# Retention rounds of a hybrid decoder step: one transpose of decayed queries and keys per tile, score and state products of an output bank in groups of four

## The reference

```python
def retention_chunk(S_prev, qkv):
    q, k, v = qkv
    L = q.shape[1]
    ...
    decay = jnp.where(diff[None] >= 0, jnp.exp(lg[:, None, None] * jnp.maximum(diff, 0.0)[None]), 0.0)
    ...
    scores = jnp.einsum('blhd,bmhd->bhlm', qf, kf) * decay[None]
    intra = jnp.einsum('bhlm,bmhe->blhe', scores, vf)
    cross = jnp.einsum('blhd,bhde->blhe', qf, S_prev) * jnp.exp(lg[None, :] * (i[:, None] + 1.0))[None, :, :, None]
    kdec = kf * jnp.exp(lg[None, :] * (L - 1.0 - i)[:, None])[None, :, :, None]
    S_new = jnp.exp(lg * L)[None, :, None, None] * S_prev + jnp.einsum('blhd,blhe->bhde', kdec, vf)
    return S_new, intra + cross
```

## Time and profile before

| what | us |
|---|---|
| median of 3 runs | 2623.97 |
| lowest, highest | 2623.03, 2638.55 |
| the profiled execution, own time | 2633.68 |
| its span in the trace | 2631.9 |
| its mean granted TensorE clock | 0.926 |
| TensorE busy in matmuls | 2323.4 (88%) |

### The profile page before, as it was taken

The page is one execution under the profiler, slowest core; times in us unless marked ns, Lnnn a source line. Parts: engine busy times, 40 slices in busy tenths (PEclk is TensorE's granted clock), DMA queues, the critical chain, the costliest instruction groups (busy, mean ns, idle before and its releaser), DMA issues. The chain is left out here.

```text
span 2631.9 us, 33747 instructions
## 1 busy us (share of the span) xinstructions
PE 2323.4 (88%) x11448; PEld 1881.9 (72%) x11448; DVE 953.9 (36%) x1497; ACT 945.3 (36%) x1483; POOL 660.5 (25%) x392
## 2 busy tenths in 40 slices
PE   6999999738999965999999659789889999994899
PEld 6988988736777754776676348667768778883787
DVE  3333333432367455777777400121121113211000
ACT  4322223222344341776777420132212343333200
POOL 1311111011022000255465552113111231113421
PEclk9998888869999987999999779889999999997999
DMA  5121211030221012899999353332221223214431
GB/s 141 33 45 45 48 44 44 26 78 10 49 57 25 1 25 91 291 317 319 312 312 319 115 170 108 110 113 105 98 87 51 67 92 108 67 35 136 143 98 59
DMA packets 258356, 289.12 MB, mean 110 GB/s; under 512 B 66955, under 2 KB 169741, under 8 KB 258125
## 3 DMA queue, kind: packets, MB, share of 16 engines
q1 hardware_dynamic: 240988, 254.22, 31.2%
q10 hardware_dynamic: 17264, 33.59, 3.5%
HBM read 247.47 MB, written 41.32 MB: 110 GB/s over the span
## 5 line engine op out<-in xcount | busy, mean ns | idle before, releaser
L209 PE MATMUL bank<-whi,x_hi 128*128 128x512 f32 (+1 forms) x1536 | 591.1, 385 | 42.9 <-POOL wlo L189 21.4
L211 PE MATMUL bank<-wlo,x_hi 128*128 128x512 f32 (+1 forms) x1536 | 581.8, 379 | 0.0
L213 PE MATMUL bank<-whi,x_lo 128*128 128x512 f32 (+1 forms) x1536 | 580.6, 378 | 0.0
L209 PEld LDWEIGHTS bank<-whi,x_hi 128*128 128x128 f32 x1536 | 294.3, 192 | 101.5 <-issue 37.1
L242 ACT ACTIVATE projected<-bank 128x512 f32<-128x512 f32 (+1 forms) x192 | 107.2, 563 | 704.0 <-PE bank L213 686.4
L213 PEld LDWEIGHTS bank<-whi,x_lo 128*128 128x128 f32 x1536 | 294.3, 192 | 41.6
L211 PEld LDWEIGHTS bank<-wlo,x_hi 128*128 128x128 f32 x1536 | 295.1, 192 | 39.5 <-issue 0.7
L1808 POOL TENSOR_TENSOR dec_v_lo<-dec_v,dec_v_hi 128x1024 fp32r<-128x1024 f32 x96 | 237.4, 2494 | 238.5 <-ACT dec_v_hi L2110 238.4
L189 POOL TENSOR_TENSOR wlo<-wraw,whi 128x512 fp32r<-128x512 f32 (+1 forms) x192 | 228.8, 1222 | 12.6 <-ACT whi L182 12.6
L1946 DVE TENSOR_TENSOR dec_kt_lo<-bank,dec_kt_hi 128x512 fp32r<-128x512 f32 x256 | 171.5, 685 | 98.2 <-ACT dec_kt_hi L2100 97.7
L2100 ACT ACTIVATE dec_kt_hi<-bank 128x512 fp32r<-128x512 f32 x256 | 150.9, 596 | 92.9 <-PE bank L1831 81.4
(11 more groups left out here) (310 smaller groups left out, 3686.8 us busy)
## 6 DMA issues: line engine op xcount, KB each, us to landing
dec_k<-cache_k SPq DMA_DIRECT2D x256, 256.0 KB, 3.9
dec_v<-cache_v SPq DMA_DIRECT2D x256, 256.0 KB, 4.2
wraw<-w_in_even SPq DMA_DIRECT2D x32, 512.0 KB, 5.9
wraw<-w_in_odd SPq DMA_DIRECT2D x16, 1024.0 KB, 8.1
gv<-projected ACTq DMA_DIRECT2D x4, 2304.0 KB, 8.1
gm_v<-gv SPq DMA_DIRECT2D x8, 1152.0 KB, 5.8
m<-gm_mt ACTq DMA_DIRECT2D x8, 1056.0 KB, 4.1
wraw<-w_in_odd SPq DMA_DIRECT2D x4, 2048.0 KB, 8.6
```

The lines of the kernel that those rows point to most:

```text
L209: pe.matmul(bank[:, 0:width], e.xhi[:, k, c:c + P], e.whi[:, k, 0:width], start=(k == 0), stop=False)
L211: pe.matmul(bank[:, 0:width], e.xhi[:, k, c:c + P], e.wlo[:, k, 0:width], start=False, stop=False)
L213: mm = pe.matmul(bank[:, 0:width], e.xlo[:, k, c:c + P], e.whi[:, k, 0:width], start=False, stop=(k == KD - 1))
```

## The change

The decayed queries and decayed keys are now written side by side into one tile `qk`, 128 columns for each of the nine tiles, and one transpose per tile turns both: 9 transposes instead of 27, four to a bank. Keys come out on partitions 64 to 127 and are copied down to 0 to 63. Scores are made from decayed keys and decayed queries; the decay table becomes a constant per head under the causal mask, which takes the surplus factor out. The use numbers of the banks are given by names, 16 uses instead of 22. The state contributions stand before the scores, on TensorE and on VectorE. An output bank takes its four score products, then its state products. A round begins only when both halves of `qk` are written (`rotated` counts to 2).

```diff
         rot = sb("rot", [P, TT, 2, DK])
-        qd = sb("qd", [P, TT, DK])
-        kd = sb("kd", [P, TT, DK])
+        qk = sb("qk", [P, TT, 2, DK])
         kd_own = sb("kd_own", [NS, DB, DK])
-        tr = sb("tr", [DK, TT, 3, P])
+        q_turned = sb("q_turned", [DK, TT, P])
+        k_turned = sb("k_turned", [DK, TT, P])
...
-        rotated = c.begin("rotated", 1)
-        k_decayed = c.begin("k_decayed", 1)
-        own_ready = c.begin("own_ready", 1)
+        rotated = c.begin("rotated", 2)
...
-        mb = Banks(c, 3, e.banks[3:8], 22)
+        use_turn, use_turn_s = (0, 1), 2
+        use_scores, use_scores_s = (3, 4), 5
+        use_state, use_state_s = (6, 7), (8, 9)
+        use_out, use_out_s = (11, 12), 10
+        use_m, use_m_s = (13, 14), 15
+        mb = Banks(c, 3, e.banks[3:8], 16)
...
+                    pe.wait_ge(rotated.sem, rotated.at(r, 2))
+                    for half, u in enumerate(use_turn):
                         pe.wait_ge(mb.read(u), mb.read_before(r, u))
...
+                        for i in range(4):
+                            mm = pe.transpose(mb.bank(u)[:, P * i:P * i + P],
+                                              qk[:, 4 * half + i + 1, :, :].rearrange("p a f -> p (a f)"), e.ident[:])
+                        mm.then_inc(mb.written(u), 1)
+                    pe.wait_ge(mb.read(use_turn_s), mb.read_before(r, use_turn_s))
+                    alone(pe, e)
+                    pe.transpose(mb.bank(use_turn_s)[:, 0:NS], qk[0:NS, 0, :, :].rearrange("p a f -> p (a f)"),
+                                 e.ident[0:NS, 0:NS]).then_inc(mb.written(use_turn_s), 1)
+                    pe.wait_ge(values_ready.sem, values_ready.at(r, 1))
+                    for half, u in enumerate(use_state):
                         pe.wait_ge(mb.read(u), mb.read_before(r, u))
...
                         for i in range(4):
...
+                            t = 4 * half + i + 1
+                            mm = pe.matmul(mb.bank(u)[0:DK, P * i:P * i + P], qk[:, t, 1, :], values[:, t, :],
                                            start=True, stop=True)
                         mm.then_inc(mb.written(u), 1)
...
+                    for half, u in enumerate(use_scores):
                         pe.wait_ge(mb.read(u), mb.read_before(r, u))
...
+                        pe.wait_ge(mb.read(use_turn[half]), mb.read_by(r, use_turn[half]))
                         for i in range(4):
...
+                            t = 4 * half + i + 1
+                            mm = pe.matmul(mb.bank(u)[:, P * i:P * i + P], k_turned[:, t, :], q_turned[:, t, :],
                                            start=True, stop=True)
                         mm.then_inc(mb.written(u), 1)
...
+                    u = use_scores_s
+                    pe.wait_ge(mb.read(u), mb.read_before(r, u))
+                    pe.wait_ge(mb.read(use_turn_s), mb.read_by(r, use_turn_s))
+                    alone(pe, e)
+                    pe.matmul(mb.bank(u)[0:NS, 0:NS], k_turned[:, 0, 0:NS], q_turned[:, 0, 0:NS],
+                              start=True, stop=True).then_inc(mb.written(u), 1)
+                    pe.wait_ge(own_ready.sem, own_ready.at(r, 2))
+                    for half, u in enumerate(use_state_s):
                         pe.wait_ge(mb.read(u), mb.read_before(r, u))
...
                         alone(pe, e)
                         for i in range(4):
...
+                            mm = pe.matmul(mb.bank(u)[0:DK, P * i:P * i + P], kd_own[:, 4 * half + i, :],
                                            values[0:NS, 0, :], start=True, stop=True)
                         mm.then_inc(mb.written(u), 1)
...
+                    pe.wait_ge(mb.read(use_scores_s), mb.read_by(r, use_scores_s))
                     pe.wait_ge(state_landed.sem, state_landed.at(r, 32))
...
+                    u = use_out_s
+                    pe.wait_ge(mb.read(u), mb.read_before(r, u))
                     alone(pe, e)
...
+                    pe.matmul(mb.bank(u)[0:NS, 0:DV], sc_s[:], values[0:NS, 0, :], start=True, stop=False)
                     for b in range(DB):
...
+                        mm = pe.matmul(mb.bank(u)[0:NS, 0:DV], qd_own[:, b, :], state_in[:, b, :],
                                        start=False, stop=(b == DB - 1))
...
+                    mm.then_inc(mb.written(u), 1)
+                    for half, u in enumerate(use_out):
                         pe.wait_ge(mb.read(u), mb.read_before(r, u))
...
+                        pe.wait_ge(mb.read(use_scores[half]), mb.read_by(r, use_scores[half]))
                         for i in range(4):
...
+                            t = 4 * half + i + 1
+                            pe.matmul(mb.bank(u)[:, P * i:P * i + P], sc[:, t - 1, :], values[:, t, :],
+                                      start=(i == 0), stop=False)
+                        pe.wait_ge(mb.read(use_state[half]), mb.read_by(r, use_state[half]))
+                        for i in range(4):
+                            t = 4 * half + i + 1
                             if t > 1:
...
+                                mm = pe.matmul(mb.bank(u)[:, P * i:P * i + P], q_turned[:, t, :], states[:, t - 2, :],
+                                               start=False, stop=(i == 3))
                         mm.then_inc(mb.written(u), 1)
...
+                    dve.tensor_tensor(qk[:, :, 0, :], rot[:, :, 0, :], qdh, ALU.mult).then_inc(rotated.sem, 1)
+                    dve.tensor_tensor(qk[:, :, 1, :], rot[:, :, 1, :], kdh, ALU.mult).then_inc(rotated.sem, 1)
+                    dve.wait_ge(rotated.sem, rotated.at(r, 2))
+                    dve.tensor_tensor(kd_own[:], qk[0:NS, 0, 1, :].unsqueeze(1).broadcast_to([NS, DB, DK]),
                                       own_batch[:].unsqueeze(2).broadcast_to([NS, DB, DK]),
...
+                                      ALU.mult).then_inc(own_ready.sem, 1)
+                    u = use_turn[0]
+                    dve.wait_ge(mb.written(u), mb.written_by(r, u))
+                    dve.tensor_copy(k_turned[:, 1:5, :], mb.bank(u)[DK:2 * DK, :].rearrange("p (t c) -> p t c", t=4))
+                    dve.tensor_copy(q_turned[:, 1:5, :], mb.bank(u)[0:DK, :].rearrange("p (t c) -> p t c", t=4)).then_inc(
+                        mb.read(u), 1)
+                    u = use_turn_s
+                    dve.wait_ge(mb.written(u), mb.written_by(r, u))
+                    dve.tensor_copy(k_turned[:, 0, 0:NS], mb.bank(u)[DK:2 * DK, 0:NS])
+                    dve.tensor_copy(q_turned[:, 0, 0:NS], mb.bank(u)[0:DK, 0:NS]).then_inc(mb.read(u), 1)
+                    dve.wait_ge(mb.read(u), mb.read_by(r, u))
+                    dve.tensor_tensor(qd_own[:], q_turned[:, 0, 0:NS].unsqueeze(1).broadcast_to([DK, DB, NS]),
+                                      own_batch_t[:], ALU.mult).then_inc(own_ready.sem, 1)
+                    dve.wait_ge(state_stored.sem, state_stored.at(r, 0))
...
+                    for half, u in enumerate(use_scores):
+                        dve.wait_ge(mb.written(u), mb.written_by(r, u))
+                        dve.tensor_tensor(sc[:, 4 * half:4 * half + 4, :], mb.bank(u)[:].rearrange("p (a c) -> p a c", a=4),
+                                          decay[:, ds(r * P, P)].unsqueeze(1).broadcast_to([P, 4, P]),
+                                          ALU.mult).then_inc(mb.read(u), 1)
+                    u = use_scores_s
+                    dve.wait_ge(mb.written(u), mb.written_by(r, u))
+                    dve.tensor_tensor(sc_s[:], mb.bank(u)[0:NS, 0:NS], decay_s[:, ds(r * NS, NS)],
+                                      ALU.mult).then_inc(mb.read(u), 1)
...
+                    u = use_turn[1]
+                    act.wait_ge(mb.written(u), mb.written_by(r, u))
+                    act.activation(k_turned[:, 5:9, :], mb.bank(u)[DK:2 * DK, :].rearrange("p (t c) -> p t c", t=4), ACT.Copy)
+                    act.activation(q_turned[:, 5:9, :], mb.bank(u)[0:DK, :].rearrange("p (t c) -> p t c", t=4),
+                                   ACT.Copy).then_inc(mb.read(u), 1)
+                    u = use_out_s
...
-    dec = np.where(diff[:, None, :] >= 0, np.exp(lg[None, :, None] * np.maximum(diff, 0)[:, None, :]), 0.0)
-    out["c_decay"] = (dec * DK ** -0.5).reshape(P, H * P).astype(f)
+    dec = np.where(diff[:, None, :] >= 0, np.exp(-lg * P)[None, :, None], 0.0)
+    out["c_decay"] = dec.reshape(P, H * P).astype(f)
     d4 = lane[None, :] - lane[:, None]
     own = (batch[:, None] == batch[None, :])
-    dec = np.where((own & (d4 >= 0))[:, None, :], np.exp(lg[None, :, None] * np.maximum(d4, 0)[:, None, :]), 0.0)
-    out["c_decay_s"] = (dec * DK ** -0.5).reshape(NS, H * NS).astype(f)
+    dec = np.where((own & (d4 >= 0))[:, None, :], np.exp(-lg * DL)[None, :, None], 0.0)
+    out["c_decay_s"] = dec.reshape(NS, H * NS).astype(f)
     qd = np.zeros((P, H, TT))
     kd = np.zeros((P, H, TT))
     qd[:, :, 1:] = np.exp(lg[None, :] * (tok[:, None] + 1.0))[:, :, None]
```

(19 more changed lines are left out.)

120 lines of the change are left out of this document (28 added, 92 removed).

## The result

| | before | after |
|---|---|---|
| median of the runs | 2627.88 us (2623.03 to 2638.55, 4 runs) | 2735.72 us (2734.32 to 2739.11, 4 runs) |
| ratio | | 1.0412, 95% interval 1.0385 to 1.0438 |
| profiled execution, its span | 2633.68, 2631.9 | 2736.61, 2734.8 |
| mean granted clock | 0.926 | 0.894 |
| first load of the next block (L594 on SyncE) | 564.88 | 667.56 |

The account below looks back on a forecast made before the run. TensorE's chain and its falling clock were taken to bound the rounds, SyncE's last gather the block's end. Work and waits -8, clock +18, round 7 +3 gave +13 on 2624: 2637 us, range 2610 to 2662.

Parts of the forecast that it names:

- SyncE's queue: End of the retention block: the last gather ends last, by 1.2 us, and hangs on round 6's sums.
- Transposes: TensorE, start of each round: nine transposes in 1.1 us instead of 27 in 2.92; gain 1.8 us.
- Output grouping: TensorE's chunk outputs: fewer changes of kind take a round from 6.06 to 4.1 us; gain 2.0, bounds 0 to 2.7.
- rival D: Output products: grouping does not save, outputs stay at 6.06 us; +27, 2651 us; chance 0.08.
- Idle before L767: TensorE waits before the state products for ScalarE's copy of the second transpose bank; 1.2 us, bounds 0.7 to 1.6.
- Idle before L789: TensorE waits before the sample contributions for VectorE to free bank6; 1.0 us, bounds 0.5 to 2.5; round 0 up to 2.5 more.
- The clock: TensorE in rounds 0 to 6: rounds 0 and 6 fall too, others earlier; +18 us, bounds -36 to +35.
- the 6 us for the other five rounds: Rounds 1 to 5: clock falls 2 to 3 us earlier, costing 1.2 us each, 6 together.
- the clock term: The +18 us for lower clock, expected from thin work and idle growing from some 5 to 7 us a round.
- A: Rival: clock falls as before, rounds 0 and 6 hold; -8, 2616 us; chance 0.22.
- B: Rival: clock gets better and the five falls go; -44, 2580 us; chance 0.05.
- C: Rival: clock falls at a round's start, whole rounds at half clock in most heads; +33, 2657 us; chance 0.15.

Follow-up runs that it names:

- e1: Changed kernel with SyncE's wait ahead of the state load naming use 12 instead of 18; 2649.0 us, ratio 1.0099.
- e3: Kernel before with only the output products of a bank grouped, four score products, then the state products; 2593.4 us, ratio 0.9901.
- e5: e1 with VectorE's masked sample queries made after the sample scores, awaited by TensorE only ahead of the sample outputs; 2651.3 us, ratio 1.0076.
- e4: e1 with other banks: state contributions in uses 3 and 4, scores in 5 and 6, sample scores in 7; 2628.4 us, ratio 1.0009.
- e7: e1 with the chunk outputs tile by tile again, score product then state product; 2673.7 us, ratio 1.0158.
- e6: Edits of e4 and e5 together: load wait mended, other banks, sample queries late; 2624.1 us, ratio 0.9977.
- e10: e6 with extra overwritten transposes, four ahead of the sample contributions and eight ahead of the sample outputs; 2595.1 us, ratio 0.9868.
- e8: e3 with eight extra overwritten transposes a round between the sample contributions and the sample outputs; 2594.4 us, ratio 0.9872.
- e9: Control to e8: the same eight extra transposes placed ahead of the state contributions, 3.8 us earlier; 2609.6 us, ratio 0.9935.

## Why the prediction was wrong, step by step

- **The step that failed: SyncE's queue.** The prediction used it for the end of the block alone ("It hangs on the sums of round 6") and took the position of the state loads for given, so the sum has no term for it. It listed waits that the change adds on TensorE, VectorE and ScalarE. It did not ask which waits keep their text and change their meaning when the uses are numbered anew. This step is worth 86.7 us of the 108 (e1) and came with its own second effect, half clock after each 15 us of idle. None of the rivals had it. The rows of `load_state` (L696 before) were in the trace in the middle of each projection, 20 us ahead of the turn (152.63 against 172.31).
- **Transposes.** Eight in 0.97 us and the small one in 0.24 (from 117.53 and 118.50): 1.2, forecast 1.1. Right.
- **Output grouping.** 4.12 us for 4.1: the price of the products is right, and rival D, that grouping doesn't save, falls. The term of 14 us for seven rounds is too small all the same: e3 won 33.4, for it also lost three of the five falls.
- **Idle before L767.** 1.36 in round 0 and 1.04 to 1.11 after, forecast 1.2 within 0.7 to 1.6. Right. **Idle before L789.** 1.16 in five of the six later rounds of e1, forecast 1.0 (in the profile after only round 6 has it, the others run at half clock there or nearly); in round 0 3.43, forecast 1.0 + 2.5. Right, and its cause is the one named, VectorE's product beside GpSimd's split. The row itself says only "issue"; e5 shows the cause:

```profile
120.02 3.63 DVE L878 TENSOR_TENSOR ret_qd_own<-ret_q_turned,ret_own_batch_t 64x256 f32<-64x256 f32 x1
...
127.61 3.64 PE L789 MATMUL bank<-ret_values,ret_kd_own 32*64 32x128 f32 x16 [3.43 <-issue]
...
135.29 2.07 PE L807 MATMUL bank<-ret_values,ret_sc 128*128 128x128 f32 x8
137.29 1.65 PE L813 MATMUL bank<-ret_states,ret_q_turned 64*128 64x128 f32 x6
...
142.88 0.69 PE L209 MATMUL bank<-whi,x_hi 128*128 128x392 f32 x1
```

- **The clock.** Rounds 0 and 6 fell too, as forecast (126.0 and 600.5 in the profile after): round 0 took 25.35 us (117.53 to 142.88) where it had taken 17.1. The sign was right. But the 6 us for the other five rounds are not there. In rounds 1 to 4 of e1 the fall came 9.9 to 10.6 us into the round, against 9.9 to 11.2 in rounds 1 to 5 before, and lasted 13.6 or 13.7 us, where most had lasted 17. In e4, which has less idle, it came 7.1 us into round 1.
- **The sum without the fault.** e1 stands for it: +22 by the medians, 17 to 35 by the interval, where the sum said +13, so even this part was too small. That it came so near is in part luck, for two errors cancel. The grouping won 33 (e3), not 14. The rest of the change cost about 45 (e7 against before) or 56 (e1 against e3), where the forecast without its grouping term comes to 13 + 14 = 27. The idles were sized rightly, so what was too small is most likely the clock: e3 falls in two rounds of its profile, e1 in all seven.
- **The reason behind the clock term.** "The forecast is wrong if [...] the idle before L789 is absent, since the clock term rests on it": e4 took that idle away in rounds 1 to 5 and the falls stayed; in e6 round 0 had no idle but 0.41 us ahead of the sample outputs and fell all the same, at 125.1. So the falls do not need that idle, as the five of the kernel before, which had none there, say too. Nor is idle shown to play no part: most falls of e4 lie inside a new idle, and in e10 only the two rounds with 2.2 us of it fell. What is shown is that dense 128-row work in the thin stretch keeps the clock and the same work 3.8 us earlier does not (e8 against e9). The change removes 18 transposes of 128 rows ahead of that stretch. Whether this or the new idle made rounds 0 and 6 fall stays open; no run put exactly those 18 back.
- **Rivals.** A (clock as before) falls with rounds 0 and 6, B (clock better) with every round. C, at half clock from the start of a round, did happen in five rounds, but through the 16 us of idle and not through the one of 1.2. In e1 one round was near it: round 5 fell at 433.9, 2.8 us in, just behind the idle before L767, came back at 437.3 and fell again at 440.7:

```profile
433.46 3.29 PE L767 MATMUL bank<-ret_values,ret_qk 128*64 128x128 f32 x16 [1.11 <-ACT ret_q_turned L953]
```

  For B the prediction cited the Trainium skill (TensorE: Matmul & The Clock Gate, Part 4, PE-mode transpose), by which transposes do not count as busy in the same way. By that, eight added transposes would have kept no clock. This case's trace does not agree: measured against e9, the transposes of e8 did keep it, where they stand in the thin stretch (2594.4 against 2609.6 us). The measurement decides, for these transposes of float32.
- **Slips in the working.** VectorE's steps to free bank6 add up to 7.2 us, not 7.4 (3.5 + 0.4 + 2.68 + 0.64). The slow output row of 1.22 us stands in four of rounds 1 to 5; in round 3 it is 1.13. The 5 us for round 6 are 1 more than the two terms named for it. None of them changes the outcome.

The late load had no cover: SyncE's issue, the load, the split, the copies of the turn and the freeing of its bank follow one another. Before, the 20 us of projection between the issue and the turn hid the first two; behind the turn nothing hides them.

## What to carry to other kernels

When bank uses, buffer slots or counters are numbered anew, go through every wait that names one by a literal, on the DMA queue's engine first: such a line does not show in the diff, and what it still guards it may guard much later than needed. Before trusting a sum of small terms, follow each load that the block needs back to the wait that lets it go, and see how much time lies between. And where the clock falls in a stretch of products with few rows, dense work put into that stretch can be cheaper than a fall (1.0 us a round against 5 to 7 for each fall). It pays only if most rounds fall: on e3, with two falls left, it gained nothing. Merging the transposes saves 1.7 us of work a round, but with the waits and the order that came with it it cost some 50 us, so price what a saving does to the clock with an experiment of its own.

## What the runs showed of the hardware that was not expected

- Eight float32 transposes, 1.0 us, hold the clock at 1.00 through seven rounds when they stand between the sample contributions and the sample outputs, and not when they stand 3.8 us earlier (one profile of each; the runs, 2591 to 2597 us against 2607 to 2616, agree). Why rounds of one kernel that look alike differ (1, 3 and 4 fell in e9, 1 and 2 in e3) stays open.
- VectorE's product of two tiles in SBUF beside a series of GpSimd instructions: it took 0.40 us alone, and in some rounds 2.7 to 3.7 (2.82, 3.63 after, 3.68 in e6, twice 3.67 in e10, 2.66 to 2.68 five times in e5), although one of GpSimd's eight splits takes 0.98. These long ones ended 0.28 or 0.29 us after the last of the eight had ended: before 123.79 against 123.51, after 123.65 against 123.36, and in e10 293.72 against 293.44, from this row of GpSimd:

```profile
285.64 7.80 POOL L189 TENSOR_TENSOR wlo<-wraw,whi 128x392 fp32r<-128x392 f32 x8
```

  So the product can wait for the whole rest of a series, where the prediction weighed the wait for one instruction. It does not always: in rounds 1 to 5 of the kernel before it stood inside the same series and took 1.31 us once and 0.56 to 0.58 four times, as in round 2:

```profile
242.53 0.57 DVE L875 TENSOR_TENSOR ret_qd_own<-ret_tr,ret_own_batch_t 64x256 f32<-64x256 f32 x1
...
241.78 8.03 POOL L189 TENSOR_TENSOR wlo<-wraw,whi 128x392 fp32r<-128x392 f32 x8
```

  What decides between the two stays open. VectorE's recurrence and score products, which read a bank, took the same beside the series as without it (0.34 us in all 56 cases, 0.67 to 0.69 in all 16).
